# Second block's attentions: keys 0 to 127 alone for the first token tile, and a 384-column layout

## The reference

```python
causal = key_pos[None, :] <= t[:, None]
# dsa (6 heads, one key head): 64 keys are picked per token by an index score, among the causal ones
score_idx = jnp.where(causal[None], einsum('bqh,bqhs->bqs', wb, relu(q_idx . k_idx)), -jnp.inf)
_, sel = lax.top_k(score_idx, 64)
p = softmax(where(sel <= t, q . k, -inf));  y_a = p @ v
# diff (4 heads, two half-width score sets): a = softmax(s0) - lam * softmax(s1);  y_b = a @ v
# moba (6 heads; with 256 tokens its one block is plain causal attention): y_c = softmax(s) @ v
x = x + gt1 * (concat(y_a, y_b, y_c) @ w_out)
```

## Time and profile before

| what | value |
|---|---|
| timed runs, median (lowest to highest) | 1915.73 us (1909.13 to 1918.5), 3 runs |
| profiled execution, first to last instruction (its span) | 1912.1 us |
| granted TensorE clock, mean over the span | 0.983 |
| attentions of the third layer (index scores to start of the output projection's last tiles) | about 664 to 755 us |
| the same of the fourth layer | about 1004 to 1096 us |

### The profile page before, as it was taken

The page is one execution under the profiler, slowest core; times in us unless marked ns, Lnnn a source line. Parts: engine busy times, 40 slices in busy tenths (PEclk is TensorE's granted clock), DMA queues, the critical chain, the costliest instruction groups (busy, mean ns, idle before and its releaser), DMA issues.

```text
span 1912.1 us, 26024 instructions
## 1 busy us (share of the span) xinstructions
PE 1824.1 (95%) x8799; PEld 1486.2 (78%) x8799; DVE 1416.6 (74%) x1631; ACT 1122.6 (59%) x1296; POOL 392.8 (21%) x315
## 2 busy tenths in 40 slices
PE   7899999989999998899989879999999999999997
PEld 6678886868888786688878667888888888888885
DVE  5748874466976586644458758889888888888897
ACT  6745444564443464443345537777777777777775
POOL 3722203463212363200046500000000000000000
PEclk9999999999999999999999989999999999999999
DMA  8348884418987341455544258999999999999994
GB/s 271 111 161 327 343 342 147 149 54 323 344 347 275 91 152 45 154 195 179 192 154 142 69 187 334 386 376 386 380 384 376 383 383 381 380 374 381 381 387 167
DMA packets 237934, 506.45 MB, mean 265 GB/s; under 512 B 23304, under 2 KB 74720, under 8 KB 231712
## 3 DMA queue, kind: packets, MB, share of 16 engines
q1 hardware_dynamic: 225664, 492.91, 70.9%
q0 software_dynamic: 3008, 10.32, 2.0%
q10 hardware_dynamic: 9184, 2.23, 0.5%
HBM read 497.49 MB, written 7.91 MB: 264 GB/s over the span
## 4 chain that ended last, share of the span: by engine, by line
PE 83%; DVE 7%; issue 6%; ACT 3%; POOL 1%; DMA 0%; POOLq 0%; SPq 0%; DVEq 0%; ACTq 0%
PE bank L2351 25%; PE bank L2353 25%; PE bank L2352 25%; PE bank L2470 2%; ACT slab L2042 1%; PE bank L2789 1%; DVE slab L1290 1%; PE bank L2561 1%; PE bank L2539 1%; ACT w_hi L1892 1%; PE bank L2521 1%; POOL w_lo L826 1%; DVE x L1074 0%; PE bank L2572 0%; DVE slab L1271 0%
## 5 line engine op out<-in xcount | busy, mean ns | idle before, releaser
L977 DVE TENSOR_TENSOR w_lo<-slab,w_hi 128x2048 fp32r<-128x2048 f32 x369 | 847.8, 2308 | 214.3 <-ACT w_hi L1892 213.3
L1892 ACT ACTIVATE w_hi<-slab 128x2048 fp32r<-128x2048 f32 (+2 forms) x421 | 796.6, 1898 | 329.0 <-PE bank L2353 256.3
L2351 PE MATMUL bank<-w_hi,hT_hi 128*128 128x512 f32 (+3 forms) x1664 | 649.4, 390 | 14.2 <-DVE hT_lo L1012 4.4
L2352 PE MATMUL bank<-w_lo,hT_hi 128*128 128x512 f32 (+3 forms) x1664 | 638.0, 383 | 0.0
L2353 PE MATMUL bank<-w_hi,hT_lo 128*128 128x512 f32 (+3 forms) x1664 | 637.9, 383 | 0.0
L2351 PEld LDWEIGHTS bank<-w_hi,hT_hi 128*128 128x128 f32 x1664 | 316.0, 190 | 77.9 <-DVE w_lo L977 8.8
L2353 PEld LDWEIGHTS bank<-w_hi,hT_lo 128*128 128x128 f32 x1664 | 315.5, 190 | 59.7
L2352 PEld LDWEIGHTS bank<-w_lo,hT_hi 128*128 128x128 f32 x1664 | 316.3, 190 | 55.3
L826 POOL TENSOR_TENSOR w_lo<-slab,w_hi 128x512 fp32r<-128x512 f32 (+2 forms) x208 | 262.4, 1295 | 381.3 <-ACT w_hi L1892 361.6
L2351 PE MATMUL bank<-w_hi,hid_hi 128*128 128x512 f32 x680 | 265.6, 391 | 0.7 <-DVE w_lo L977 0.7
L2353 PE MATMUL bank<-w_hi,hid_lo 128*128 128x512 f32 x680 | 265.0, 390 | 0.0
(11 more groups left out here) (252 smaller groups left out, 1232.0 us busy)
## 6 DMA issues: line engine op xcount, KB each, us to landing
slab<-in_w_exp_gate SPq DMA_DIRECT2D x176, 512.0 KB, 7.0
slab<-in_w_exp_up SPq DMA_DIRECT2D x176, 512.0 KB, 7.5
slab<-in_w_exp_down SPq DMA_DIRECT2D x176, 512.0 KB, 7.1
slab<-in_w_ada SPq DMA_DIRECT2D x48, 1024.0 KB, 5.5
slab<-in_w_mlp_in SPq DMA_DIRECT2D x64, 512.0 KB, 5.4
slab<-in_w_mlp_out SPq DMA_DIRECT2D x64, 512.0 KB, 9.0
slab<-in_w_in SPq DMA_DIRECT2D x56, 512.0 KB, 5.0
slab<-in_w_out SPq DMA_DIRECT2D x32, 512.0 KB, 4.6
```

The lines of the kernel that those rows point to most:

```text
L977: dve.tensor_tensor(w_lo[:, q, 0:n], raw(s)[:, 0:n], w_hi[:, q, 0:n].bitcast(F32), ALU.subtract).then_inc(lo_dve, 1)
L1892: act.activation(w_hi[:, q, 0:n], raw(s)[:, 0:n], ACT.Copy).then_inc(hi_done, 1)
L2351: pe.matmul(dst, a_hi, b_hi, start=start, stop=False)
L2352: pe.matmul(dst, a_hi, b_lo, start=False, stop=False)
```

## The change

In the second block alone, tile 0 now covers keys 0 to 127, which are all that its tokens may see; tile 1 covers keys 0 to 255 as before. Scores, masks, picks, probabilities and their transposes have 128 + 256 = 384 columns instead of 512. In detail:

- the scores' and index scores' matmuls of tile 0 have 128 columns, its masks, exponentials, searches and replacements too;
- the transposes lose one of four (tile 0's second half), so a diff head has three and a pair six; copies of their banks have 384 columns;
- `values` of a diff head has three matmuls instead of four; of a pair, the matmuls of the second half of the keys cover tile 1's 128 columns;
- since a broadcast over unequal tiles can't be written, a pair's multiplication by the row's reciprocal is two instructions per set (tensor_scalar, 128 and 256 columns) instead of one (tensor_tensor, 512 columns); the first product of the index scores becomes a tensor_scalar as well.

```diff
+SEEN_AT, SEEN_W = (0, P), (P, SEQ)
+SEEN = sum(SEEN_W)
...
+        def seen(t, a):
+            return a[:, SEEN_AT[t]:SEEN_AT[t] + SEEN_W[t]]
+        def sp_row(l, s, u, t):
+            if l < DEPTH:
+                return sp_set(s, u)[:, t]
+            return seen(t, scr(X_SP + ((2 * u + s) % 4) * COL, SEEN))
+        def score_row(l, b, t):
+            return bank[b][:, t * SEQ:(t + 1) * SEQ] if l < DEPTH else seen(t, bank[b])
+        def pt_width(l):
+            return COL if l < DEPTH else SEEN
... masked_max
-                            to = sp_set(s, u)[:, t]
-                            src = bank[SC[j % 3]][:, t * SEQ:(t + 1) * SEQ]
+                            to = sp_row(l, s, u, t)
+                            src = score_row(l, SC[j % 3], t)
... normalise
                         for t in range(TT):
-                            dve.scalar_tensor_tensor(p0[:, t], p1[:, t], r[:, 1, t:t + 1], p0[:, t], ALU.mult, ALU.add
-                                                     ).then_inc(nrm_done, 2)
+                            p0, p1 = sp_row(l, 0, u, t), sp_row(l, 1, u, t)
+                            dve.scalar_tensor_tensor(p0, p1, r[:, 1, t:t + 1], p0, ALU.mult, ALU.add).then_inc(nrm_done, 2)
...
-                            dve.tensor_tensor(p, p, r[:, s, :].unsqueeze(2).broadcast_to([P, TT, SEQ]), ALU.mult).then_inc(nrm_done, 2)
+                            for t in range(TT):
+                                p = sp_row(l, s, u, t)
+                                dve.tensor_scalar(p, p, r[:, s, t:t + 1], None, ALU.mult).then_inc(nrm_done, 1)
... second_out (and ACT's first_out, second_out alike)
-                    dve.tensor_copy(pt_set(1), bank[PT[1]][:, :]).then_inc(ptb_done, 1)
+                    w = pt_width(l)
+                    dve.tensor_copy(pt_set(1)[:, 0:w], bank[PT[1]][:, 0:w]).then_inc(ptb_done, 1)
... index scores and picks
-                                mark(dve.tensor_tensor(selw[:, t], r[:, t], w.broadcast_to([P, SEQ]), ALU.mult))
+                                mark(dve.tensor_scalar(seen(t, selw), seen(t, r), w, None, ALU.mult))
-                            picked[t] = mark(dve.max(m8, selw[:, t]))
+                            picked[t] = mark(dve.max(m8, seen(t, selw)))
... scores
-                                            qkT[r, k, :], start=True, stop=True)
+                                            qkT[r, k, :] if l < DEPTH else qkT[r, k, 0:SEEN_W[t]], start=True, stop=True)
... turn_scores
-                            for t in range(TT):
-                                o = k * SEQ + t * P
+                            for t in range(0 if l < DEPTH else k, TT):
+                                o = k * SEQ + (t if l < DEPTH else t - k) * P
... values
-                            for k in range(TT):
+                            for k in range(t + 1):
+                            late = 0 if l < DEPTH else k * P
...
-                                                prj[:, k, vc[s]:vc[s] + HD], pt_set(s)[:, k * SEQ:(k + 1) * SEQ],
+                                                prj[:, k, vc[s]:vc[s] + HD], pt_set(s)[:, k * SEQ:(k + 1) * SEQ - late],
```

More of the change, by code:

```diff
@@ L67 @@
 F_WIDE = 512
+SEEN_AT, SEEN_W = (0, P), (P, SEQ)
+SEEN = sum(SEEN_W)
 _at = {}
 _n = 0
-for _name, _w in (("ident", P), ("ones", P), ("before", P), ("iota", P), ("dilated", TT * SEQ), ("causal", TT * SEQ),
+for _name, _w in (("ident", P), ("ones", P), ("before", P), ("iota", P), ("dilated", TT * SEQ), ("causal", SEEN),
                   ("ax_cos", TT * HD), ("ax_sin", TT * HD), ("pr_cos", TT * 16), ("pr_sin", TT * 16),
@@ L118, in constants @@
     put("dilated", by_token(bias))
-    put("causal", by_token(np.where(k <= q, 0.0, MASKED)))
+    causal = np.where(k <= q, 0.0, MASKED)
+    put("causal", np.concatenate([causal[t * P:(t + 1) * P, 0:SEEN_W[t]] for t in range(TT)], 1))
     def rope(pos, half, theta):
@@ L1276, in normalise @@
                     r = att[:, 3, 2 * u:2 * u + 2, :]
-                    p0, p1 = sp_set(0, u), sp_set(1, u)
                     if is_diff(l, u):
@@ L1434, in _ @@
                         n = idx_done[0] = idx_done[0] + 1
-                        r = scr(X_SP, TT * SEQ, TT, SEQ)
+                        r = scr(X_SP, SEEN)
                         dve.wait_ge(ix_done, n)
-                        dve.tensor_scalar(r, bank[IX_BANKS[i]][:, :].rearrange("p (t n) -> p t n", t=TT),
+                        dve.tensor_scalar(r, bank[IX_BANKS[i]][:, 0:SEEN],
                                           HD ** -0.5 * I2 ** -0.5, 0.0, ALU.mult, ALU.max).then_inc(ixe_done, 1)
@@ L2048, in first_out @@
                     act.wait_ge(av_done, U0 + u)
-                    act.activation(pt_set(0), bank[PT[0]][:, :], ACT.Copy).then_inc(pta_done, 1)
+                    w = pt_width(l)
+                    act.activation(pt_set(0)[:, 0:w], bank[PT[0]][:, 0:w], ACT.Copy).then_inc(pta_done, 1)
                 def second_out(u):
                     act.wait_ge(ptb_t, pairs_before(l, u) + 1)
-                    act.activation(pt_set(1), bank[PT[1]][:, :], ACT.Copy).then_inc(ptb_done, 1)
+                    w = pt_width(l)
+                    act.activation(pt_set(1)[:, 0:w], bank[PT[1]][:, 0:w], ACT.Copy).then_inc(ptb_done, 1)
                 def y_high(u):
@@ L2520, in scores @@
                             r = slice(base, base + dims)
[L2521 to L2522 removed]
+                            ins = pe.matmul(score_row(l, SC[(2 * u + s) % 3], t), qkT[r, q, t * P:(t + 1) * P],
+                                            qkT[r, k, :] if l < DEPTH else qkT[r, k, 0:SEEN_W[t]], start=True, stop=True)
                             if t == TT - 1:
@@ L2663, in _ @@
                         for t in range(TT):
-                            ins = pe.matmul(bank[IX_BANKS[i]][:, t * SEQ:(t + 1) * SEQ], qkT[s, i // 2, t * P:(t + 1) * P],
-                                            qkT[s, 2, :], start=True, stop=True)
+                            ins = pe.matmul(seen(t, bank[IX_BANKS[i]]), qkT[s, i // 2, t * P:(t + 1) * P],
+                                            qkT[s, 2, 0:SEEN_W[t]], start=True, stop=True)
                         ins.then_inc(ix_done, 1)
```

35 lines of the change are left out of this document (19 added, 16 removed).

## The result

| | before | after |
|---|---|---|
| median (lowest to highest) | 1911.37 us (1909.13 to 1918.5), 5 runs | 1903.16 us (1900.79 to 1905.39), 5 runs |
| ratio, 95% interval | | 0.9948, 0.9930 to 0.9966 |
| once more, other runs | 1911.64 us, 17 runs | 1902.86 us, 5 runs: 0.9963, 0.9950 to 0.9976 |
| span of the profiled execution | 1912.1 us | 1901.4 us |

The change wins some 8 us, 0.4 to 0.5%. The forecast had 1.1 us. Its number, 1914.6, is 11.4 us too high: 4 us of that is the median of three runs it started from (1915.73, against 1911.4 and 1911.6 with more runs), the other 7 us is the effect.

The account below looks back on a forecast made before the run. PE bounds most of the run, DVE and ACT the attention stages' middle. Per layer -0.9 us, twice -1.8, with the clock -1.1: 1914.6 us; own range 1910 to 1918, 8 in 10 from 1903 to 1921.

Parts of the forecast that it names:

- index scores to unit 3's masks: Stage's start, to 702 us: narrower PE passes save 0.9 and PE's 0.78 us wait goes; -1.6 us per layer.
- unit 3 and its picks: Narrower masks, join and searches win, but copies waiting for POOL give the masks' gain back; -0.4 us per layer.
- unit 4, under POOL: Unit 4's normalising during POOL's eight splits: six port waits on DVE instead of four; +1.4 us per layer.
- units 5 to 7 and unit 8's masks, to POOL's start on tile 15: POOL rests, so narrower masks, scalings, copy and exponentials win; -2.0 us per layer.
- POOL's start to `out_tile` 0: Unit 8's scalings wait four times for POOL, +2.45; transposes and values behind win 0.2; +2.25 us per layer.
- last part: Unit 9's transposes, values of units 8 and 9 and ACT's two narrower copies, all on PE's path; -0.57 us.
- the middle part: 702 to 744 us, DVE and ACT bound; under POOL each DVE scaling waits for a split (1.25 us) and delays the next.
- the other estimate: The Trainium skill's DVE table: a set's two new scalings take 0.32 us instead of 0.59, saving 1.6 us more over the run.
- The clock: At unit 8's end PE's longer gap may lower the third layer's clock, 1.35 us; half taken once, +0.7.
- B: Rival: the new scalings pass POOL without waiting; -8.4 us per layer, 1899 us; chance 0.15.
- C: Rival: unit 4's scalings meet one more split each (1.25 us), and both layers get the low clock; 1919 us; chance 0.21.
- D: Rival: half-wide instructions save nothing because a fixed part carries them; 1919 to 1923 us; chance 0.06.

Follow-up runs that it names:

- wide_pe: Changed kernel with tile 0's scores and index scores at 256 columns again and an unread transpose added for the dropped one; 1904.05 us, one execution.
- before_again: The kernel before, profiled once more with no edit; 1915.01 us, one execution.
- one_scale: Changed kernel with a pair's scaling as one multiplication of 384 columns per set instead of two instructions; 1895.54 us, ratio to before 0.9921.
- late_split: Changed kernel with POOL starting tiles 15 and 16 after unit 9's scalings instead of after unit 8's masks; 1893.45 us, ratio 0.9917.
- one_gated: Changed kernel with one multiplication per set, POOL's tile 13 after unit 7's scalings and tiles 14 to 16 after unit 9's; 1895.99 us, ratio 0.9926.
- halves_before: Kernel before at 512 columns, with each pair's multiplication split into two tensor_scalars of 256 columns; ratio 1.0007.

## Why the forecast was wrong

Step by step, in us, between the milestones named; the last column is the mean of both layers in both profiled executions of each kernel:

| step | forecast | third layer, first profiles | mean of the four stages |
|---|---|---|---|
| index scores to unit 3's masks | -1.6 | -2.1 | -2.1 |
| unit 3 and its picks | -0.4 | -1.0 | -1.0 |
| unit 4, under POOL | +1.4 | +0.95 | +0.95 |
| units 5 to 7 and unit 8's masks, to POOL's start on tile 15 | -2.0 | -2.2 | -2.2 |
| POOL's start to `out_tile` 0 | +2.25 | +2.0 | +1.3 |
| last part | -0.6 | -1.65 | -1.4 |
| sum | -0.9 | -4.0 | -4.45 |

The mechanism was right: narrower instructions win, DVE's second port wait takes part of it back. The sign of every step was right too. What failed is that -0.9 was a small remainder of +3.65 and -4.6, and all the errors fell on one side. The largest part of them lies at the port.

- **The failed step: the middle part, where "POOL's next then waits for it" was priced for any instruction alike.** The forecast let a scaling cost the split (1.25) and its own time (0.20 or 0.27), four in 5.94 us. From POOL's start at 734.41 to the end of unit 8's second pair (737.16 + 2.38) it took 5.13, four splits of 1.25 and hardly more: the split behind a tensor_scalar starts as if it weren't there. That is 0.8 us too much at unit 8, and the mean of the four stages is 0.95 under the forecast there. In the first profiles only 0.25 of it is to be seen, because of the clock (below). At unit 4 POOL's stretch is 10.20 us long where it was 11.74 (710.61 to 722.35): 0.64 of the difference is the pause ahead of its last four splits, which is gone, the other 0.9 is POOL no longer held up as much. With its earlier start it ends at 718.56 where the forecast had it end at 720.65; DVE left at 719.0, not at 720.6. (The forecast's words, "with the last split but one", do not go with its number: that split would have ended at about 719.4. DVE did leave behind the last one.) The quiet pairs were priced well: 0.55 us, less the overlap of 0.08, is the 0.47 of the sum and not the 0.32 of the other estimate.
- **Unit 3's copies give nothing back.** The forecast had POOL take the gain there. DVE now reaches the rotary embedding (L1220) at 702.34, before POOL's splits begin at 702.60: two instructions take 0.45 us where they took 2.07, behind POOL's start at 704.53. A phase again; with what the copies behind lose, the step wins 0.6 us more than forecast. Timelines of DVE and POOL before, then after:

```profile
704.74 2.07 DVE L1198 TENSOR_TENSOR h<-big,rope 128x112 f32<-128x112 f32 x2
...
704.53 4.24 POOL L826 TENSOR_TENSOR w_lo<-slab,w_hi 128x384 fp32r<-128x384 f32 x4 [7.00 <-ACT w_hi L1892]
```

```profile
702.34 0.45 DVE L1220 TENSOR_TENSOR h<-big,rope 128x112 f32<-128x112 f32 x2
...
702.60 4.07 POOL L848 TENSOR_TENSOR w_lo<-slab,w_hi 128x384 fp32r<-128x384 f32 x4 [6.50 <-ACT w_hi L1920]
```

- **PE's passes** were sized from other instructions. A narrow score or index pass saves 0.05 us (2.10 to 1.68 for the index scores' eight), not 0.02; a pair's values save 0.21, not 0.07. That is 0.3 us in the last part. In the first part, which is 0.5 under the forecast, wide_pe puts 0.8 us (third layer) and 1.3 (fourth) on the widths for which the sum had 0.7, so PE's passes are 0.1 to 0.6 of the miss there. The transposes' price held (1.03 to 0.82: 0.21 against 0.22).
- **The clock** had been weighed at unit 8's end alone, but it fell in two places. PE's timeline and window at unit 9's values, before:

```profile
749.60 1.03 PE L2539 MATMUL bank<-const,slab 128*128 128x128 f32 x8
750.57 1.08 PE L2561 MATMUL bank<-slab,big 128*64 128x256 f32 x8
753.73 1.46 PE L2561 MATMUL bank<-slab,big 128*64 128x256 f32 x8 [2.07 <-DVE hT_lo L1308]
```

```profile
754.00:758.00 4.00, 4.00 (x15) 2.67 (x12) 0.42 (x1) 0.38 (x1) 0.00 (x0) 0.57 1.07 351
```

Two windows of the changed kernel, at unit 8's end and at the work of the window above, and PE's values of unit 7:

```profile
740.00:744.00 4.00, 4.00 (x17) 2.76 (x16) 3.77 (x13) 2.88 (x11) 4.00 (x4) 0.57 0.02 4
751.50:755.50 4.00, 4.00 (x22) 3.21 (x23) 0.42 (x1) 0.39 (x1) 0.00 (x0) 1.00 0.17 55
```

```profile
740.09 1.55 PE L2592 MATMUL bank<-slab,big 128*64 128x256 f32 x8
```

Before, PE stands idle for 2.07 us ahead of the values of unit 9, and is granted 0.57 behind them: 15 matmuls in 4 us. After, it idles for 1.86 and is granted 1.00: 22 matmuls. In return the changed kernel falls to half at unit 8's end, where the third layer of before had 1.00, a fall that the forecast had priced at 1.35 us and put into the sum by half. At half clock 3.4 us (754.3 to 757.7) cost 1.6 us of weight matmuls, one each 0.43 us for 0.227. Of the other fall 1.8 us lie behind `out_tile` 0's start and cost 0.8; the rest lies ahead of it, where the values of unit 7 take 1.55 us instead of 0.87 (748.73). So in the first profiles the last part has 0.8 us from the clock, and the step ahead of it loses 0.7. The second executions and the fourth layer show which of this stays. The fall behind unit 9's values is in all four stages of before and in none of the changed kernel's. The fall at unit 8's end is in all four of the changed kernel's and in three of the four of before: the first profile's third layer, from which the forecast was made, is the one without it. In before_again the same place is granted 0.57:

```profile
745.00:749.00 4.00, 3.91 (x15) 2.27 (x16) 3.67 (x14) 3.20 (x11) 4.00 (x3) 0.57 0.00 0
```

By the mean of the stages the forecast lacked 3.5 us per layer: 0.5 + 0.6 + 0.45 + 0.2 + 0.95 + 0.8, step by step. The price of the port is the largest piece (0.45 at unit 4 and most of the 0.95 at unit 8), and the phase at unit 3 (0.6) is a meeting with POOL as well. How much of the last two steps is the clock in the mean was not taken apart. The measured 1903.2 lies below the forecast's own range (1910 to 1918); that it lies just inside the wide one is luck, since the low end of that allowed for a part-way B, and B did not come. Of the rivals, B (no added wait) is out by the pairs of 2.4 us, though on the other engine's side the tensor_scalars do go nearly unnoticed: POOL isn't held up. C (slower) and D (half-wide instructions save nothing) are out by the milestones. The Trainium skill (SBUF — State Buffer, SBUF: two separate sides) lets whichever starts first, a GpSimd instruction or a DVE instruction in a two-port mode or with two SBUF inputs, have the shared ports for its whole instruction, the other blocked. The scalings' waits agree with it; POOL's side does so in part for a tensor_tensor, not measurably for these tensor_scalars (last section).

Outside the two stages the forecast allowed no change; the 2.7 us behind the router are the clock's, by before_again.

## What to carry to other kernels

Where two engines take turns at a port, count an instruction's turns, not its columns: a scaling cut in two won 25% of its columns and lost 0.9 to 1.0 us for each added turn (a pair of 2.4 us where one multiplication took 1.3 to 1.5), and writing it as one (one_scale) or moving the other engine's work past it (late_split) won 7.6 and 9.7 us, about as much again as the change itself. A forecast that is a small remainder of large opposite terms has the error of the terms, so its range must be that of their sum; check first which of them meet in a phase, since what one engine wins ahead of such a meeting can be gone behind it (wide_pe). A second profile of the kernel before, taken ahead of the forecast, would have shown which steps of a stage repeat and which hang on the clock. And an engine taken out of one bound's way meets the next (one_gated, where PE's weights bound at once).

## What the runs showed of the hardware

How long POOL is held up depends on the kind of DVE instruction and, for a tensor_tensor, on its width. Eight splits of tiles 15 and 16 take 9.93 us with none among them (late_split). With four multiplications of 512 columns they take 11.76, of 384 columns 11.20, with four pairs of tensor_tensors (128 and 256) 10.54, with four pairs of tensor_scalars 10.03 (128 and 256) or 10.17 (256 twice, halves_before). Per multiplication or pair that is 0.46, 0.32, 0.15, 0.03 and 0.06 us; the fourth layer gives the same totals within 0.03 us. DVE itself waits for the running split in all these cases.

The granted clock differs between executions of the same code: 0.78 and 0.94 over the same 29.8 us behind the router; from the router to the end these two executions differ by 4 us (781.9 and 777.9).
